# A GLA layer in fp32 products: two blocks' MLPs as one stage of 1024 tokens with one Strassen level

## The reference

```python
h = rms_norm(x, norm_mix[i])
m = rms_norm(mem, norm_mem[i])
y_mix, xq = gla_branch(h, gla_w_in[j], gla_w_gate2[j], gla_b_gate[j], gla_out_gain[j])
y_mem = memory_cross_attention(xq, m, w_kv[i])
x = x + jnp.concatenate([y_mix, y_mem.astype(y_mix.dtype)], axis=-1) @ w_out[i]
u = jax.nn.relu(rms_norm(x, norm_mlp[i]) @ w_up[i])
x = x + (u * u) @ w_down[i]
return rms_norm(x, final_norm)
```

## Time and profile before

| | us |
|---|---|
| median of 3 runs | 2464.06 (2461.39 to 2465.43) |
| the profiled execution's span | 2459.9 |
| median above the span | 4.2 |
| PE busy | 2441.6 (99%) |
| DVE busy | 1830.7 (74%) |
| ACT busy | 1291.8 (53%) |
| GpSimd busy | 312.5 (13%) |
| moved by DMA | 505 MB, 205 GB/s on the mean |

### The profile page before, as it was taken

The page is one execution under the profiler, slowest core; times in us unless marked ns, Lnnn a source line. Parts: engine busy times, 40 slices in busy tenths (PEclk is TensorE's granted clock), DMA queues, the critical chain, the costliest instruction groups (busy, mean ns, idle before and its releaser), DMA issues.

```text
span 2459.9 us, 34497 instructions
## 1 busy us (share of the span) xinstructions
PE 2441.6 (99%) x12912; PEld 2105.9 (86%) x12912; DVE 1830.7 (74%) x2671; ACT 1291.8 (53%) x2035; POOL 312.5 (13%) x327
## 2 busy tenths in 40 slices
PE   9999999999999999999999999999999999999998
PEld 8888888888788888889988888898898888889987
DVE  6677468778856788777775768877785677887777
ACT  5545354544543456566644345665665435556655
POOL 0033200000303320000020431000020142000000
PEclk9999999999999999999999999999999999999999
DMA  8964548677695444466564626355665553545554
GB/s 317 350 213 172 188 172 313 251 274 258 244 373 211 171 163 133 163 214 209 188 219 175 242 101 202 111 184 203 213 212 203 189 199 122 184 149 177 188 182 179
DMA packets 237843, 505.00 MB, mean 205 GB/s; under 512 B 12432, under 2 KB 125456, under 8 KB 219504
## 3 DMA queue, kind: packets, MB, share of 16 engines
q1 hardware_dynamic: 237248, 502.73, 58.4%
q10 hardware_dynamic: 432, 0.07, 0.0%
HBM read 423.07 MB, written 79.69 MB: 204 GB/s over the span
## 4 chain that ended last, share of the span: by engine, by line
PE 95%; DVE 2%; DMA 2%; issue 1%; ACT 0%; POOL 0%; SPq 0%; DVEq 0%; POOLq 0%; ACTq 0%
PE banks L3026 28%; PE banks L3028 28%; PE banks L3027 28%; PE banks L3216 3%; PE banks L3188 1%; PE banks L3262 1%; PE banks L3256 1%; PE banks L3165 1%; PE banks L3240 1%; DMA sr<-in_w_out 1%; PE banks L3178 0%; PE banks L3482 0%; PE banks L3274 0%; DMA xres<-in_x 0%; PE banks L3099 0%
## 5 line engine op out<-in xcount | busy, mean ns | idle before, releaser
L3026 PE MATMUL banks<-h_hi,w_hi 128*128 128x512 f32 (+1 forms) x1728 | 605.6, 350 | 2.4 <-DMA w_lo<-w_in_lo 0.8
L3028 PE MATMUL banks<-h_hi,w_lo 128*128 128x512 f32 (+1 forms) x1728 | 598.1, 346 | 0.0
L3027 PE MATMUL banks<-h_lo,w_hi 128*128 128x512 f32 (+1 forms) x1728 | 597.9, 346 | 0.0
L2833 DVE TENSOR_TENSOR w_lo<-raw,w_hi 128x1024 fp32r<-128x1024 f32 (+1 forms) x312 | 364.8, 1186 | 56.7 <-ACT w_hi L1861 56.4
L1861 ACT ACTIVATE w_hi<-raw 128x1024 fp32r<-128x1024 f32 (+1 forms) x312 | 300.9, 1003 | 166.7 <-PE banks L3026 59.4
L3026 PEld LDWEIGHTS banks<-h_hi,w_hi 128*128 128x128 f32 x1728 | 327.3, 189 | 44.1 <-issue 3.1
L3028 PEld LDWEIGHTS banks<-h_hi,w_lo 128*128 128x128 f32 x1728 | 327.2, 189 | 40.6
L3027 PEld LDWEIGHTS banks<-h_lo,w_hi 128*128 128x128 f32 x1728 | 327.5, 190 | 39.3
L3026 PE MATMUL banks<-w_hi,u_hi 128*128 128x512 f32 x896 | 350.8, 392 | 1.3 <-ACT w_hi L1401 1.0
L3028 PE MATMUL banks<-w_hi,u_lo 128*128 128x512 f32 x896 | 348.8, 389 | 0.0
L3027 PE MATMUL banks<-w_lo,u_hi 128*128 128x512 f32 x896 | 348.7, 389 | 0.0
(11 more groups left out here) (311 smaller groups left out, 4392.9 us busy)
## 6 DMA issues: line engine op xcount, KB each, us to landing
raw<-w_mix SPq DMA_DIRECT2D x52, 1024.0 KB, 4.8
raw<-in_w_down SPq DMA_DIRECT2D x48, 1024.0 KB, 5.7
raw<-w_up_mix SPq DMA_DIRECT2D x72, 512.0 KB, 4.8
w_hi<-w_in_hi SPq DMA_DIRECT2D x29, 1024.0 KB, 4.9
w_lo<-w_in_lo SPq DMA_DIRECT2D x29, 1024.0 KB, 7.9
raw<-in_w_up SPq DMA_DIRECT2D x28, 1024.0 KB, 5.6
raw<-in_gla_w_in SPq DMA_DIRECT2D x21, 1024.0 KB, 7.5
raw<-in_w_up SPq DMA_DIRECT2D x36, 512.0 KB, 4.1
```

The source lines that it names most:

```text
L2833: nc.vector.tensor_tensor(w_lo[:, i % 2, at], raw[:, i % 2, at], w_hi[:, i % 2, at].bitcast(F32), ALU.subtract).then_inc(lo_split.sem, 1)
L3026: after_chunk(pe.matmul(to, left[0], right[0], start=start, stop=False, skip_group_check=goes_on))
L3027: pe.matmul(to, left[0], right[1], start=False, stop=False, skip_group_check=goes_on)
L3028: return pe.matmul(to, left[1], right[0], start=False, stop=stop, skip_group_check=goes_on)
```

## The change

The two mixers of an even and an odd block now run one behind the other, and then one MLP on both, `MLPS = 2` stages of 1024 tokens. The even block's tokens are half 1, the odd block's half 2.

- **Up stage.** All 16 chunks use one Strassen level on halves of 512 tokens: `UP_STEPS`, 112 steps of 4 × 3 matmuls of 512 columns. `UP_ORDER` is M1, M2, M5, M6, M7, M3, M4 and `up_bank` gives M1, M6, M7 and M4 one bank, M5 and M3 another, M2 a third; the first three chunks are interleaved. ACT's high part of w_up runs six steps ahead in a ring (`up_high`), DVE's low part five (`up_low`), and DVE makes w_up's T sums each time (`up_sum`); `w_up_mix` is gone. Sums of h are made at the stage's begin (`s_sums`, `s_high`, `s_low`). `make_u` (ACT) squares, `u_sums` (DVE) makes S1 to S4 of u, and `store_u`, `store_u_sums` write the seven operands of each chunk to `u_kept` in DRAM (0.75 and 1 MB).
- **Down stage.** `DOWN_STEPS`, 28 steps of a product's quarter of the hidden columns, 48 matmuls each; a product adds up in PSUM over four quarters. Each step loads 1 MB of weights and 1 MB of u, and ACT and DVE split both again.
- **w_down's sums** are made by GpSimd: `half_mix_sums`, 32 half mixes of four 128x256 subtractions, in the first up stage alone. SP loads and stores them between the other transfers, and waits for `half_mix_made` and `half_mix_stored`.
- **Out-projection** of block 0 is by Strassen too (252 matmuls in place of 288), with six sums of w_out and the sums of y made in block 0.
- **Kept in DRAM**: `h_kept` (the even block's h, transposed), `x_kept` (residual rows), each stored before the MLP and read back for it. Block 0 loads its own and the second block's rows early (2 MB), block 1 stores rows and columns (2 MB each).

The diff has some 3300 changed lines. Its core is below; of the three loops over `UP_STEPS` after `half_mix_sums`, the first is ACT's, the second DVE's, and `up_product` is PE's.

```diff
+MLPS = BLOCKS // 2
+FIRST_UPS = 3
+UP_ORDER = ("M1", "M2", "M5", "M6", "M7", "M3", "M4")
+UP_STEPS = [(c, name) for c in range(FIRST_UPS) for name in ("M1", "M2")]
+UP_STEPS += [(c, name) for name in ("M5", "M6") for c in (2, 1, 0)]
+UP_STEPS += [(c, name) for c in (2, 1, 0) for name in ("M7", "M3", "M4")]
+UP_STEPS += [(c, name) for c in range(FIRST_UPS, UPS) for name in UP_ORDER]
+UP_LEAD = 5
+UP_ENDS = {15: 2, 20: 1, 25: 0, 30: 3, 36: 4, **{UP_AT[c, "M4"] + 1: c for c in range(5, UPS)}}
+DOWN_STEPS = [(name, quarter) for name, _, _, _ in PRODUCTS for quarter in range(QUARTERS)]
+DOWN_BANKS = {"M1": 0, "M6": 0, "M7": 0, "M4": 0, "M5": 4, "M3": 4, "M2": 4}
+DOWN_MIX = 2 * UPS
+DOWN_MIX_AT = {18 + 5 * j // 2: j for j in range(DOWN_MIX)}
...
+def up_bank(c, name):
+    if name == "M2":
+        return 6 + c % 2
+    turn = c if c < FIRST_UPS else (5 - c) % 3
+    return turn + (3 if name in ("M5", "M3") else 0)
...
+            def half_mix_load(j):
+                slot, c, half = j % 2, j // 2, slice(j % 2 * 256, (j % 2 + 1) * 256)
...
+                    sp.wait_ge(half_mix_stored[slot], 16 * (j // 2))
+                for k in range(2):
+                    sp.dma_start(half_mix[:, slot, 2 * k:2 * k + 2, :],
+                                 wdown[:, 2 * c + k, :].rearrange("p (d c) -> p d c", d=2)[:, :, half])\
+                        .then_inc(half_mix_loaded[slot], 16)
+            def half_mix_store(j):
...
+                sp.wait_ge(half_mix_made, j + 1)
+                sp.dma_start(w_mix[:, c // DEPTH, :, c % DEPTH, half], half_mix[:, slot]).then_inc(half_mix_stored[slot], 16)
...
+            def load_mlp(m):
+                load_up(m, 2)
+                store_rows(2 * m + 1)
+                for at in range(len(UP_STEPS)):
...
+                    for c in range(FIRST_UPS, UPS - 2):
+                        if at == UP_AT[c, "M4"] - UP_LEAD:
+                            load_up(m, c + 2)
+                    if at - 1 in UP_ENDS:
+                        store_u(m, UP_ENDS[at - 1])
+                    if at - 3 in UP_ENDS:
+                        store_u_sums(m, UP_ENDS[at - 3])
+                    if m == 0 and at + 3 in DOWN_MIX_AT:
+                        half_mix_load(DOWN_MIX_AT[at + 3])
+                    if m == 0 and at - 1 in DOWN_MIX_AT:
+                        half_mix_store(DOWN_MIX_AT[at - 1])
...
+            def half_mix_sums(j):
+                b11, b12, b21, b22 = (half_mix[:, j % 2, e, :] for e in range(4))
+                pool.wait_ge(half_mix_loaded[j % 2], 32 * (j // 2 + 1))
+                nc.gpsimd.tensor_tensor(b11, b12, b11, ALU.subtract).then_inc(mix_first, 1)
+                pool.wait_ge(mix_first, j + 1)
+                nc.gpsimd.tensor_tensor(b12, b22, b12, ALU.subtract)
+                nc.gpsimd.tensor_tensor(b22, b22, b11, ALU.subtract).then_inc(mix_third, 1)
+                pool.wait_ge(mix_third, j + 1)
+                nc.gpsimd.tensor_tensor(b21, b21, b22, ALU.subtract).then_inc(half_mix_made, 1)
...
+                for at, (c, name) in enumerate(UP_STEPS):
+                    if UP_LEAD < at + UP_LEAD + 1 < len(UP_STEPS):
+                        up_high(m, at + UP_LEAD + 1)
+                    if at in S_HIGHS_AT:
+                        s_high(S_HIGHS_AT[at])
+                    if name in ("M1", "M5", "M6"):
+                        keep_part(c, name)
+                    if at in UP_ENDS:
+                        make_u(UP_ENDS[at])
...
+                for at, (c, name) in enumerate(UP_STEPS):
+                    for e in S_SUMS_AT.get(at, ()):
+                        s_sums(e)
+                    if at + UP_LEAD < len(UP_STEPS):
+                        up_low(m, at + UP_LEAD)
+                    if at in S_LOWS_AT:
+                        s_low(S_LOWS_AT[at])
+                    if name in ("M2", "M7", "M3"):
+                        add_part(c, name)
+                    if at - 2 in UP_ENDS:
+                        u_sums(UP_ENDS[at - 2])
...
+                def up_product(s):
+                    c, name = UP_STEPS[s]
...
+                    pe.wait_ge(*mlp_empty(m, ("up", c, name)))
+                    high, low = up_operand[operand]
+                    to = bank(("up", c, name))
+                    for k in range(KG):
+                        last = product(to, (ring_hi[:, s % RING, k, :], ring_lo[:, s % RING, k, :]),
+                                       (high[:, k, :], low[:, k, :]), begins and k == 0, k == KG - 1, not begins)
+                    last.then_inc(bank_full[bank_of(("up", c, name))], 1)
```

More of the change, by code:

```diff
@@ L159 @@
[L159 to L172, removed]
@@ L197, with __init__ @@
 V_ROWS = {(0, 0): "M2", (0, 1): "M3", (1, 0): "M4", (1, 1): "M7"}
-V_SUMS = (S1, S2, S3, S4)
+STATE_STEPS = {8: [("kT", 0)], 9: [("su", 0), ("o", 0)], 10: [("kT", 1)], 11: [("su", 1), ("o", 1)],
+               12: [("kT", 2)], 13: [("su", 2), ("o", 2)]}
+ROWS_AT = 8
 class Signal:
[L204 to L209, removed]
+    def __init__(self, sem, before, per_phase, step=1):
+        self.sem, self.before, self.step = sem, before, step
+        self.per_phase = per_phase if isinstance(per_phase, list) else [per_phase] * BLOCKS
     def at(self, n, k):
[L213 to L216, removed]
+        return self.sem, (self.before + sum(self.per_phase[:n]) + k + 1) * self.step
     def early(self, k):
@@ L738, in build, with bank_count @@
         dve_step = sem("dve_step")
+        mix_first = sem("mix_first")
+        mix_third = sem("mix_third")
         ones_r = ones[:].bitcast(F32R)
-        def bank_count(n, name, more):
-            uses = layout(n).uses
-            bank, index = uses.place[name]
-            ahead = sum(layout(m).uses.count[bank] for m in range(n))
+        def bank_count(phase, name, more):
+            bank, index = USES[phase].place[name]
+            ahead = sum(USES[before].count[bank] for before in range(phase))
@@ L864, in mix_uses @@
         def mix_uses(j):
[L866 to L877 removed]
+            return sum(OUT_MIX_SLOT[before] == OUT_MIX_SLOT[j] for before in range(j))
@@ new lines, in slot_uses, with columns, up_load, up_parts @@
+        def slot_uses(slot):
+            return OUT_MIX_SLOT.count(slot)
+        def columns(b):
+            return columns_late if b == 2 else columns_early
+        def up_load(c):
+            return sum(up_slot(before) == up_slot(c) for before in range(c))
+        def up_parts(c):
+            return third_parts if c == 2 else raw_parts[:, c % 2]
+        def up_source(c, operand):
+            k, f = {B11: (0, 0), B21: (1, 0), B22: (1, 1), T1: (0, 0), T3: (0, 1), T2: (0, 0), T4: (1, 0)}[operand]
+            return up_parts(c)[:, KG * k:KG * (k + 1), f, :]
@@ new lines, in store_rows, with store_columns @@
+            def store_rows(n):
+                for pair in range(2):
+                    sp.wait_ge(*read(n, ("out", "M4", pair)))
+                sp.dma_start(x_kept[:, n % 2, :, :], xres[:]).then_inc(rows_stored.sem, 16)
+            def store_columns(n):
+                for half in range(2):
+                    for g in range(KD // 2):
+                        sp.wait_ge(*read(n + 1, ("kept hT", half, g)))
+                sp.dma_start(h_kept, columns_early[:]).then_inc(columns_stored.sem, 16)
@@ L2056, in _ @@
+                for t in range(TILES):
+                    act.wait_ge(*mlp_read(m, ("down", "M4", t)))
+                    if m < MLPS - 1:
+                        square(ends[1][:, t, :], "final", m, TILES + t)
                     else:
                         half_square(t, 0)
+            for n in range(BLOCKS):
+                mixers(n)
+                if n % 2:
+                    mlp(n // 2)
         @block.vector
@@ L3010, in _ @@
+                restart()
+            for n in range(BLOCKS):
+                mixers(n)
+                if n % 2:
+                    mlp(n // 2)
         @block.tensor
@@ L3620, in pe_block @@
[L3620 to L3636 removed]
+                out_chunk(c_out)
```

2647 lines of the change are left out of this document (1202 added, 1445 removed).

## The result

The changed kernel takes 2504.4 us (median of 4 runs, 2503.1 to 2506.8) against 2462.7 of the kernel before: ratio 1.0169, 95% interval 1.0154 to 1.0183. It is slower by 42 us, where 2446 us was forecast.

The account below looks back on a forecast made before the run. PE bounds the kernel: matmul count times start interval. Savings of 60.6, 8.2 and 3 against costs of 26, 6, 3.5, 2, 2, 2 and 12 give −18.3, so 2446 us; 8-in-10 range 2416 to 2488.

Parts of the forecast that it names:

- Parts 1 and 2: Fewer matmuls on PE: up stage by Strassen gains 60.6 us, block 0's out-projection with 252 for 288 gains 8.2.
- Part 4: Up stages: M7 shares M6's bank and waits for ACT's copy, 26 times 1.0 us, +26; chunk 4 +6 more.
- Chunk 4: Up stages: make_u(3) and an up_high precede the M6 copy, a wait of 4.0 us instead of 1.0, twice, +6.
- Part 6: u's operands through DRAM: the up stage's traffic fits with little to spare, down steps of 10.9 us cover theirs; cost 0.
- part 7: First up stage: GpSimd's w_down sums and their transfers in SP's queue, cycle 16.1 us against 15.3 allowed, +12 us.
- Rival B: GpSimd with DVE paces the first up stage, store(j) heading SP's queue before load_up; 2459 to 2510 us, chance 0.24.
- Part 5: Stage ends: late sums of h +3.5 us, up to down +2, even to odd block +2, block 0's denser DMA +2.
- block to block: Even block to odd block, mixer on mixer, with next_h made behind the out-projection: +2 us (−2 to 6).
- Part 3: Old PE waits that go (w_mix's first use, v behind the transition, the like): gain 3 us, other 9 us kept.
- up to down: From up to down stage, weights and buffers come late: 1 us per stage, +2 (0 to 8).
- block 0's denser transfers: Block 0's denser DMA, with its rows of 2 MB: +2 us (0 to 5).

Follow-up runs that it names:

- the version with four edits: Changed kernel with half-mix transfers spaced, M2 between M6 and M7, ACT's squares before the softmax, half of GpSimd's scaling later: 2451.5 us, 0.9959 of the kernel before.

## Why the prediction was wrong

**Right.** Parts 1 and 2: −68.8 forecast, −67.4 measured (−73 by the other grouping), with 1908 matmuls fewer. Part 4: 26 copies of M6 on the path; the undisturbed ones, twelve in the second stage and seven in the first, are each 1.00 us, as worked out. Chunk 4 waits 3.2, not 4.0. Part 6's down stage: u through DRAM costs nothing, 305.9 and 304.0 us against 28 × 10.9.

**The step that failed** is part 7, "transfers 4.1, additions 7.0, a cycle of 16.1, +12 us". The place was right, SP's one queue. Its terms were not: the additions take 3.8 (the doubled durations of the earlier trace rows were not met in this stage), and the landings 5.3 for `w_mix` and 8.6 for u's stores, where 4.1 was taken from the earlier trace rows. And the consequence was looked for behind w_up's load, with 16 us of slack. The operand with no slack is u: `make_u` waits for `store_u`, and the M6 copy is queued behind `make_u` on ACT. Measured +35 on the stage, in place of 12.

Rival B, with a chance of 0.24, has 2504 in its range of 2459 to 2510, but by luck: it wanted additions of 1.75 us, SP standing at `half_mix_made` and PE waiting for w_up. The additions took 0.89 to 1.01 us, SP stood 19 us for them against 159 for landings, and PE waited for M6's copy.

**A term that was missing:** the clock. The forecast had every stand at its own length. Most stands of about 3 us, and two of 2.1 us in the first up stage, are followed by intervals of 0.45 us, the rate of 1.2 GHz; the short excesses rose by 25.8 us, and the run with longer stands shows 1.3 us for each stand on the mean. The Trainium skill, TensorE: Matmul & The Clock Gate, Part 1, says that an idle PE falls to half rate and has to be busy again before it gets the full one; this trace agrees, and the kernel before, whose longest stand was 2.3 us, showed nothing of it.

**Part 5 was mis-sized.** The starts cost 4.7 us each and not 1.7: the bank of M2 was overlooked as the first wait, and behind it S1's low part is as late. The out-projections, priced at +2 for block to block, cost 16 (19.9 against 3.8), and leaving GpSimd's scaling out took 10 of them: beside DVE's low parts in blocks 0 and 2 it is the very case that the earlier trace rows show and that part 7 charged to the up stage. The rule cited from the Trainium skill, SBUF — State Buffer, "Who interferes with whom", agrees there (DVE's two low parts take 4.56 us beside the scaling and 2.35 without); in the first up stage the additions were worth 9 us at most.

**Part 3.** The old waits sum to 11.1 us and not to 12.4, so that 8 and not 9 were kept; this changes nothing in the sum. But block 0's mixer got a new wait of 4.5 us behind four squares of ACT, which no part had priced (it is gone in the version with four edits).

In sum, beside the −18 forecast: 23 more for the mixes (10 of them low clock), 16 for the low clock elsewhere, 6 at the starts, 14 in the out-projections, 4.5 in the first mixer. That is 4 us more than the +41 measured: small terms (chunk 4, up to down, block 0's denser transfers) came out lower than priced.

## What to carry to other kernels

When a step joins a queue that waits in order, price what is queued behind it by who waits for it with the least slack, not by the biggest load; the same transfers a step later gave 27 us. Put a product of another bank between two that share one with a copy between: 1 us for each pair otherwise. And where one engine is the bound, a stand of 3 us on it had a price beyond its length here, one of 1 us had not.

## What the runs showed of the hardware

A wait of 1.0 us leaves the granted clock at 1.00 (eleven of them in 215 us); one of 2.9 us costs 1.3 us beyond its length on the mean (eleven of them, clock 0.94). GpSimd's 128x256 subtraction takes 0.89 to 1.01 us beside a DVE that is busy 64% of the time (232.6 of 365.1 us), and DVE's 128x512 low part 0.79 in place of 0.68; beside GpSimd's eight 128x512 multiplications one after the other, as in the out-projection, DVE's 128x1024 subtraction takes 2.31 us in place of 1.22. What stays open: how the first up stage would do with three slots for the half mixes, which would give each store's landing more time before its slot is loaded again. No run tries it, and whether there is room for a third slot isn't shown.
